# The first weight chunks and x loaded in five pieces instead of seven

## The reference

```
proj = x @ w_in[l]
(aq, ak, av, aiq, aik, aiw, bq, bk, bv, cq, ck, cv, dq, dk, dv, gate_logits) = jnp.split(proj, splits, axis=-1)
o_a = dsa_attention(...)            # indexer, top-k of 128 keys, softmax attention
o_b = chunk_rel_attention(...)
o_c = window_sink_attention(...)
o_d = stick_breaking_attention(...)
y = sum over i of sigmoid(gates[i]) * (branches[i] @ w_branch[l, i])
x = layer_norm(ALPHA * x + y @ w_out[l], ln_mix_g[l], ln_mix_b[l])
hg, hu = jnp.split(x @ w_ffn_in[l], 2, axis=-1)
x = layer_norm(ALPHA * x + (jax.nn.silu(hg) * hu) @ w_ffn_out[l], ln_ffn_g[l], ln_ffn_b[l])
```

## Time and profile before

| | us |
|---|---|
| median of 3 runs | 842.61 (842.49 to 842.98) |
| the profiled execution | 842.3 |
| its span | 840.5 |
| PE busy, of the span | 829.5 (99%) |
| DVE busy | 509.4 (61%) |
| ACT busy | 353.4 (42%) |
| mean DMA rate | 101 GB/s |

### The profile page before, as it was taken

The page is one execution under the profiler, slowest core; times in us unless marked ns, Lnnn a source line. Parts: engine busy times, 40 slices in busy tenths (PEclk is TensorE's granted clock), DMA queues, the critical chain, the costliest instruction groups (busy, mean ns, idle before and its releaser), DMA issues.

```text
span 840.5 us, 10290 instructions
## 1 busy us (share of the span) xinstructions
PE 829.5 (99%) x3943; PEld 692.6 (82%) x3943; DVE 509.4 (61%) x861; ACT 353.4 (42%) x557; POOL 29.2 (3%) x75
## 2 busy tenths in 40 slices
PE   9999999999999999999999999999999999999996
PEld 6888889788888888888888988888888888888885
DVE  5559899887789888685653976433333433222237
ACT  6554656785555536525422732222222222211122
POOL 1700000000000000000000001000000000000000
PEclk9999999999999999999999999999999999999999
DMA  8352123112121221222262214222222222222202
GB/s 276 124 210 96 51 100 101 51 51 101 60 92 63 88 101 51 101 101 74 76 249 102 96 55 156 97 98 100 100 100 100 100 100 101 100 101 101 100 1 101
DMA packets 15816, 84.51 MB, mean 101 GB/s; under 512 B 1808, under 2 KB 3860, under 8 KB 7072
## 3 DMA queue, kind: packets, MB, share of 16 engines
q1 hardware_dynamic: 13472, 76.89, 25.5%
q0 software_dynamic: 2016, 6.86, 2.3%
q10 hardware_dynamic: 288, 0.20, 0.1%
HBM read 81.82 MB, written 2.13 MB: 100 GB/s over the span
## 4 chain that ended last, share of the span: by engine, by line
PE 85%; DVE 10%; ACT 2%; issue 1%; DMA 1%; SPq 0%; DVEq 0%; ACTq 0%
PE bank L1356 57%; PE bank L1595 19%; PE bank L1658 2%; PE bank L1519 2%; DVE sel L959 2%; DVE w_all L882 2%; PE bank L1506 2%; PE bank L1403 1%; DVE top L957 1%; DVE probsT L1061 1%; ACT w_all L539 1%; PE bank L1481 1%; PE bank L1483 1%; DVE probs L1064 1%; DVE probs L1048 1%
## 5 line engine op out<-in xcount | busy, mean ns | idle before, releaser
L1356 PE MATMUL bank<-x_hi,w_all 128*128 128x512 f32 x1424 | 342.5, 390 | 0.0
L1356 PEld LDWEIGHTS bank<-x_hi,w_all 128*128 128x128 f32 x1424 | 266.1, 188 | 54.9
L882 DVE TENSOR_TENSOR w_all<-raw,w_all 128x2048 fp32r<-128x2048 f32 x65 | 148.9, 2290 | 124.6 <-ACT w_all L539 101.9
L1356 PE MATMUL bank<-x_lo,w_all 128*128 128x512 f32 x712 | 180.8, 391 | 0.0
L1356 PEld LDWEIGHTS bank<-x_lo,w_all 128*128 128x128 f32 x712 | 132.2, 188 | 26.6
L539 ACT ACTIVATE w_all<-raw 128x2048 fp32r<-128x2048 f32 x45 | 86.4, 1920 | 94.6 <-PE bank L1595 85.5
L1595 PE MATMUL bank<-w_all,h_hi 128*128 128x512 f32 x352 | 96.7, 389 | 0.0
L1595 PEld LDWEIGHTS bank<-w_all,h_hi 128*128 128x128 f32 x352 | 66.0, 188 | 13.8 <-DVE w_all L1291 0.2
L1595 PE MATMUL bank<-w_all,h_lo 128*128 128x512 f32 x176 | 56.8, 389 | 0.0
L821 ACT ACTIVATE h_hi<-swi 128x512 f32 (+1 forms) x22 | 13.9, 633 | 94.2 <-DVE swi L1268 94.2
L558 ACT ACTIVATE gates<-bank 128x512 f32<-128x512 f32 x30 | 17.9, 598 | 71.5 <-PE bank L1356 64.0
(11 more groups left out here) (285 smaller groups left out, 925.2 us busy)
## 6 DMA issues: line engine op xcount, KB each, us to landing
raw<-in_stream SPq DMA_DIRECT2D x67, 1024.0 KB, 4.8
resid<-in_x POOLq DMA_DIRECT2D x1, 2048.0 KB, 10.4
xraw<-in_xT SPq DMA_DIRECT2D x6, 256.0 KB, 5.3
out<-result SPq DMA_DIRECT2D x3, 512.0 KB, 2.6
early_raw<-in_stream SPq DMA_DIRECT2D x1, 1024.0 KB, 8.7
bias_b<-bias_vectors POOLq DMA_DIRECT2D x1, 1024.0 KB, 8.2
bias_a<-bias_vectors POOLq DMA_DIRECT2D x1, 1024.0 KB, 12.0
ln_g<-in_g POOLq DMA_DIRECT2D x2, 512.0 KB, 7.8
```

Source lines behind the costliest of these rows:

```text
L882: dve.tensor_tensor(lo, raw[:, s, :], hi.bitcast(f32), ALU.subtract).then_inc(lo_ready, 1)
L1356: ins = pe.matmul(dst, lhs[a](k), rhs[b](k), start=n == 0, stop=n == n_all - 1)
```

## The change

The cut of the first two chunks and of x is now one, one, two, two and two rows.

```diff
-PIECES = [(k, k + 1) for k in range(KT - 2)] + [(KT - 2, KT)]
+PIECES = [(0, 1), (1, 2), (2, 4), (4, 6), (6, KT)]
 VALUE_PIECES = [(0, 1), (1, 2), (2, 4), (4, KT)]
```

## The result

| | before | after |
|---|---|---|
| median (runs) | 842.69 us (8) | 845.68 us (8) |
| lowest to highest | 842.24 to 843.78 | 843.45 to 845.95 |
| the profiled execution | 842.3 | 843.45 |
| its span | 840.5 | 841.6 |
| PE busy | 829.5 | 830.0 |

A forecast was written before the change was run, and what follows sets the result against it. PE was taken as the bound, busy 829.5 of 840.5 us, with its start of row 2 setting the start. A 1.3 us later start gave 843.6 from 842.3, 843.9 against the runs, put at 843.8; range 842.4 to 845.0.

The forecast's parts named there:

- The later start of row 2: In the start, PE begins x's row 2 at 11.2 us instead of 9.95, costing 1.3 us.
- the landing: The load of x's rows 2 and 3 arrives between 9.95 and 10.4 us, taken as 10.1.
- The slow stretch at 7 us: Loads moved slowly from 7 to 9.2 us, costing 1.1 us; expected to stay, forecast chance 0.62.
- the rival in which it goes: Slow loading near 7 us disappears, PE begins row 2 at 9.75 to 10.0, no change in time; chance 0.18.
- The rival in which it grows: Slow loading covers the whole new load, rows 2 and 3 land at 10.6, +1.8 us; chance 0.13.
- The instruction term: ACT's split of two x rows takes 1.06 us against 0.64 for one, 0.42 us more before PE's row 2.
- So no new wait: After row 2, PE never waits again: rows 4 and 5 ready at 14.6 us, needed at 15.3.
- The shift passes in full: The delay of PE's row 2, +1.3 us, reaches the end; PE's 1.1 us wait at 164 us absorbs nothing.
- The clock: Rival: PE's clock falls in its 2 us pause before row 2, 1.6 us more, 845.5 on the runs; chance 0.07.

The follow-up runs named there:

- lower-group: Faster executions of the changed kernel: 843.45 and 844.12 us of its first eight runs, five of 843.06 to 844.2 in 11 more.
- upper group: Slower executions of the changed kernel: six of its first eight runs, 845.18 to 845.95 us, and six of 845.3 to 845.74 in 11 more.

## Why the prediction was wrong

**The later start of row 2: right, and somewhat small.** "PE then begins row 2 at 10.1 + 1.13 = 11.2" was 11.25 in the first profile, and 11.6 to 11.9 in the three others of the same kernel. The term that is too small is the landing, "between 9.95 and 10.4": it was 10.1 to 10.8. The slow stretch at 7 us stayed, so the rival in which it goes is out. The rival in which it grows is in part true: its landing, 10.6, is in the middle of what was seen. Where the clock didn't fall, the start costs 1.3 us in the mean of the seven timed lower-group runs (843.8, the forecast's own number), or 1.9 with the filled pause.

**The instruction term: right**, 1.06 against 0.64 us in the traces; taken away by itself it gave 0.5 us in the median, with intervals that overlap.

**"So no new wait" behind it: true in the changed kernel, and for the wrong reason.** I let rows 4 and 5 land by 13.55, from one trace, and gave them 0.7 us to spare. They landed at 13.3 to 15.0 and were covered only because PE itself was late; without that they cost 1.1 us. In the execution that landed them at 15.0 they were split at 16.1, just when PE would have come to them without the fall.

**The shift passes in full: right, nearly**, as the wait at 164 us shows (1.2 us, 1.1 before): 1.28 us at 57 us are 1.15 at the end. The loss of the clock passes too: in the execution of 845.7 us the 15 products of the earlier trace rows began at 60.36, 3.5 us late, and the end was 3.4 late.

**The clock: this is the step that failed.** The text says: "It decides from the point where the pause reaches what the end shows, about 3.7 us, and mine is 2", with a chance of 0.07. The end of the kernel showed one idle time that ended in a fall, 3.7 us or more, and I took it for the least that is needed. The traces show falls 2.2 to 2.35 us behind PE's last product, in three of them, and none in three others where the pause was 1.3 to 2.0 us. The range, up to 845.0, left most of this rival's case out. With 13 of 21 executions of the changed kernel in the upper group, the rival was the likeliest case and holds the median. Its price was right: 1.6 us expected for the fall; twelve products took 1.56 us longer, and the groups lie 1.7 to 1.9 apart; 845.5 was given for this rival, 845.68 was measured. (The prediction's "1.00 (2.4 GHz) through the start" was misread: its own seven products at 0.45 us each ran at the lower rate under that 1.00.) That the fall is the cause is shown from two sides: the pause alone, without the change, brings the upper group, and filling it takes the upper group away. Why one execution has the fall and the next not stays open. In the six traces with the unfilled pause the falls go with a quick row 0 (1.7 to 1.85 us) and with a pause of 2.1 to 2.5 us, their absence with a slow row 0 and a shorter pause. The traces' records of the clock add one thing. The three rises with a fall behind them came at 5.0, 4.6 and 5.0 us and the falls at 11.85, 11.4 and 11.8, each the same time behind its rise to 0.01 us, while the time since PE's last product differs by 0.1. In the three without a fall the rise came at 6.6 to 6.9. A quick row 0 alone isn't enough for a fall either: the profile of the kernel before (rise at 4.3, pause 0.6 us) and that with only rows 4 and 5 merged (4.3, 1.7 us before row 4) have none. So the moment of the rise and the length of the pause both seem to count, which is argued from eight traces and not shown: no run set either of them by itself in steps around 2 us.

The Trainium skill, TensorE: Matmul & The Clock Gate (What you observe), says that the transition at the start moves from run to run. The traces agree: row 0's six products took 1.83 or 2.68 us in the same kernel.

## What to carry to other kernels

A wait on TensorE has two prices: its own length, and that of the clock, which is paid only in some executions. So look for such a price in the spread of the times, not in one profile: a second group of runs was the sign here. An idle time after which the clock fell says that this much is enough, not that less is safe; where a pause of 2 us is unavoidable, products on zeros in it held the clock here at a cost of 0.3 us at most in the profiles. And a pipeline's first pieces are best cut by what the consumer waits for: merging two rows made the consumer wait for the second and for a longer split, while none of what it saved was on the path.

## What was new about the hardware

- A pause of PE of about 2 us left the clock alone in some executions of a kernel and took it to 1.2 GHz for over 3 us in others, with 1.6 us lost on twelve products (4.41 against 2.85 us).
- A filled pause (eight products on zeros, or four) left none of 33 runs in the upper group; the same kernels without it had 5 of 11 and 13 of 21 in the upper group. Of the 22 runs with the loads or splits cut otherwise, all filled, one (845.17) reached its edge.
- Some issues of SP take long, and size alone isn't it. x's rows 6 and 7 took 0.52 us to issue before. In the first profile of the changed kernel the load of x's rows 2 and 3, as large (512 KB), took 0.43, and later ones up to 1.04, that one of 256 KB:

```profile
4.06 0.43 SPq L420 DMA_DIRECT2D xraw<-in_xT  x1
5.56 0.80 SPq L420 DMA_DIRECT2D xraw<-in_xT  x1
6.40 1.04 SPq L418 DMA_DIRECT2D raw<-in_stream  x1
```

  It was hidden here. Its cause stays open.

- The slow stretch of the queue near 7 us is in nearly every trace of the start: in 7 to 8 us the seven with single loads of rows 2 and 3 moved 146 to 275 GB/s and the seven with double ones 133 to 184, against 295 to 354 in 9 to 10 us. The windows of the changed kernel's first profile (last number: GB/s):

```profile
5.50:7.00 1.50, 1.50 (x5) 1.21 (x4) 1.24 (x4) 1.09 (x3) 0.00 (x0) 1.00 1.11 189
7.00:8.00 1.00, 1.00 (x6) 0.79 (x6) 0.65 (x2) 0.00 (x0) 0.00 (x0) 1.00 0.61 135
```

against 146 GB/s in 7 to 8 us before. Its cause stays open.
